# Attention stages of a two-block transformer: v as the stationary operand, and softmax division ahead of the transposes

## What is computed

```python
def mixer_a(q, k, v, qg, kg, rope):            # 8 heads, 2 kv heads, head width 64; mixer_b the same with window, bias, sink
    q = axial_rope(rmsnorm(q, qg), rope)
    k = axial_rope(rmsnorm(k, kg), rope)
        sc = jnp.einsum('bqkgd,bskd->bkgqs', qblk, k).astype(jnp.float32)
        p = jax.nn.softmax(sc, axis=-1).astype(v.dtype)
        return jnp.einsum('bkgqs,bskd->bqkgd', p, v)

def mixer_c(...):                              # 4 heads, two softmaxes each, v of width 128
    lam = (jnp.exp(jnp.sum(lq1 * lk1)) - jnp.exp(jnp.sum(lq2 * lk2)) + lambda_init)
        p = jax.nn.softmax(sc + bias[None, :, :, None], axis=-1)
        attn = p[:, :, :, 0] - lam * p[:, :, :, 1]
        return jnp.einsum('bkgqs,bskd->bqkgd', attn.astype(v.dtype), v)
    o = rmsnorm(o, subln_g) * (1.0 - lambda_init)
```

## Time and profile before

| | |
|---|---|
| three runs, median (lowest to highest) | 2922.46 us (2916.77 to 2925.27) |
| profiled execution, span | 2917.6 us |
| profiled execution, device time | not listed apart from its span |
| PE busy | 2663.8 us, 91% |
| DVE, ACT, POOL busy | 1366.9, 983.7, 189.3 us |
| a mixer, from half 3 to the next stage's transposed rows | 231.52 us, twice |

### The profile page before, as it was taken

How to read it: one execution, slowest core, us unless ns; L and a number is a source line. 1 busy time by engine, 2 the same in 40 slices (tenths; PEclk the granted TensorE clock), 3 DMA queues, 4 the chain that set the end, 5 groups by cost and what they waited for, 6 DMA issues and landing times.

```text
span 2917.6 us, 56415 instructions
## 1 busy us (share of the span) xinstructions
PE 2663.8 (91%) x24182; PEld 1779.7 (61%) x24182; DVE 1366.9 (47%) x1878; ACT 983.7 (34%) x1705; POOL 189.3 (6%) x195
## 2 busy tenths in 40 slices
PE   8999999999999999999999998899999989766666
PEld 6877877878878878875433333344778865332222
DVE  5776566877866567643100001423777773000001
ACT  4435655444446555531200100202555542000000
POOL 0102000000002000000000000002333310000000
PEclk9999999999999999999999999999999999987787
DMA  8764335776763347642899999822100017999997
GB/s 304 274 258 161 127 131 210 302 267 244 297 236 135 125 166 286 229 176 107 346 421 421 421 421 421 328 81 101 42 11 17 11 47 282 421 421 421 421 419 323
DMA packets 103997, 716.99 MB, mean 246 GB/s; under 512 B 11949, under 2 KB 14381, under 8 KB 19801
## 3 DMA queue, kind: packets, MB, share of 16 engines
q1 hardware_dynamic: 93016, 663.75, 57.8%
q10 hardware_dynamic: 10752, 49.81, 4.5%
HBM read 711.65 MB, written 1.86 MB: 245 GB/s over the span
## 4 chain that ended last, share of the span: by engine, by line
PE 61%; DMA 20%; DVE 10%; ACT 6%; issue 2%; SPq 0%; ACTq 0%; DVEq 0%
DMA weight_ring<-in_stream 20%; PE banks L2130 9%; PE banks L667 7%; PE banks L669 6%; PE banks L668 6%; PE banks L1960 3%; PE banks L2495 3%; PE banks L1103 3%; PE banks L1105 2%; PE banks L1104 2%; PE banks L2539 2%; ACT front L1371 2%; PE banks L1263 1%; PE banks L2935 1%; PE banks L2021 1%
## 5 line engine op out<-in xcount | busy, mean ns | idle before, releaser
L2130 PE MATMUL banks<-weight_ring,scratch 128*32 128x256 f32 (+1 forms) x4256 | 560.3, 507 | 148.6 <-DMA weight_ring<-in_stream 147.0
L2130 PEld LDWEIGHTS banks<-weight_ring,scratch 128*32 128x32 f32 (+1 forms) x4256 | 183.1, 129 | 505.9 <-DMA weight_ring<-in_stream 258.7
L664 DVE TENSOR_TENSOR split_high<-weight_ring,split_high 128x1024 fp32r<-128x1024 f32 x198 | 242.5, 1238 | 124.0 <-ACT split_high L659 121.8
L659 ACT CAST split_high<-weight_ring 128x1024 fp32r<-128x1024 f32 x198 | 206.8, 1052 | 272.8 <-PE banks L669 199.3
L2281 DVE TENSOR_TENSOR scratch<-scratch,banks 128x512 f32<-128x512 f32 (+1 forms) x32 | 17.8, 555 | 561.5 <-PE banks L2130 561.5
L1463 DVE TENSOR_TENSOR split_high<-weight_ring,split_high 128x1024 fp32r<-128x1024 f32 x128 | 160.2, 1262 | 160.9 <-ACT split_high L1356 160.8
L667 PE MATMUL banks<-split_high,features_low 128*128 128x512 f32 x480 | 189.9, 396 | 0.2 <-DVE resid L700 0.2
L669 PE MATMUL banks<-split_high,features_high 128*128 128x512 f32 x480 | 187.1, 390 | 0.0
L668 PE MATMUL banks<-split_high,features_high 128*128 128x512 f32 x480 | 186.8, 389 | 0.0
L1356 ACT CAST split_high<-weight_ring 128x1024 fp32r<-128x1024 f32 x128 | 133.0, 1049 | 150.1 <-PE banks L1105 144.2
L2190 ACT ACTIVATE scratch<-banks 128x512 f32<-128x512 f32 (+1 forms) x32 | 15.7, 491 | 477.7 <-PE banks L2130 477.7
(11 more groups left out here) (448 smaller groups left out, 4870.2 us busy)
## 6 DMA issues: line engine op xcount, KB each, us to landing
weight_ring<-in_stream SPq DMA_DIRECT2D x628, 1024.0 KB, 9.8
scratch<-in_kept ACTq DMA_DIRECT2D x24, 1024.0 KB, 7.6
scratch<-in_pair_rows ACTq DMA_DIRECT2D x8, 448.0 KB, 3.7
scratch<-in_kept ACTq DMA_DIRECT2D x6, 512.0 KB, 5.5
scratch<-in_lora ACTq DMA_DIRECT2D x2, 1536.0 KB, 9.3
front<-in_gain_rows ACTq DMA_DIRECT2D x5, 512.0 KB, 3.7
bias<-bias_rows SPq DMA_DIRECT2D x1, 2304.0 KB
scratch<-in_routing ACTq DMA_DIRECT2D x1, 1040.5 KB, 4.9
```

The lines of the kernel that those rows point to most:

```text
L659: act.copy(split[i % 4][0], source(i)).then_inc(*self.rounded.up())
L664: dve.tensor_tensor(lo, source(i), hi.bitcast(F32), ALU.subtract).then_inc(*self.rest.up())
L2130: last = pe.matmul(self.psum[q * M:(q + 1) * M, (GATE, UP, DOWN)[part], 0:W], left, w[j][:, q * W:(q + 1) * W], start=(k == 0), stop=(k == ...
```

## The change

On PE:
- `values` of A and B: v (128x64) is the loaded operand and the turned probabilities of four heads are streamed (512 columns): four products instead of 16. The two kv heads write to PSUM partitions 0 to 63 and 64 to 127 of bank 7. The result is already transposed, so the `turn_outs` of A and B fall away, and with them two entries of `starts` (35.5 and 49.5).
- `turn_probs` waits for `probs_normed` instead of `expd`; in C it has two groups instead of four, and `values` of C has 8 products instead of 16.

On DVE `norm_probs` is new and stands after `maxima`: in C it divides both softmaxes by their sums and combines them, in two groups; in A and B it only inverts the sums, in four groups. `outputs` of C is a plain copy; of A and B it makes the low part of the transposed outputs. On POOL sixteen groups of two `tensor_scalar` of 128x256 divide the probabilities of A and B in place. On ACT `high_outs` copies the high part after each phase of A and B, `high` and `low` of A and B fall away, the small exponentials stand ahead of the eight large ones, and C's are taken in the order 0, 4, 1, 5, 2, 6, 3, 7. `yT_hi` and `yT_lo` of A have room of their own. The host orders the rows of `w_branch` for A and B by pairs of heads.

```diff
             def turn_probs(ph):
                 fill(at_probs[ph])
-                for g in range(4):
-                    wait(pe, self.expd, 8 * ph + 2 * g + 2)
+                before = groups_before[ph]
+                for g in range(groups_of[branch_of[ph]]):
+                    wait(pe, self.probs_normed, before + g + 1)
                     if g >= 2:
-                        wait(pe, self.probs_saved, 4 * ph + g - 1)
+                        wait(pe, self.probs_saved, before + g - 1)
...
             def values(ph):
                 fill(at_values[ph])
...
+                if branch == "C":
+                    for i in range(4):
+                        if i % 2 == 0:
+                            wait(pe, self.probs_saved, before + i // 2 + 1)
+                        at = VC + P * (i // 2)
+                        for k in range(2):
+                            last = pe.matmul(self.psum[:, 7, i * P:(i + 1) * P], probsT[:, 2 * i + k, :], proj[:, k, at:at + P],
+                                             start=(k == 0), stop=(k == 1))
+                else:
+                    wait(pe, self.probs_saved, before + 4)
                     for k in range(2):
-                        last = pe.matmul(self.psum[:, bank, col:col + w], probsT[:, 2 * i + k, :], proj[:, k, at:at + w],
-                                         start=(k == 0), stop=(k == 1))
+                        for h in range(2):
+                            at = V0[branch] + HD * h
+                            last = pe.matmul(self.psum[HD * h:HD * h + HD, 7, :], proj[:, k, at:at + HD],
+                                             probsT[:, 8 * h + k:8 * h + 8:2, :], start=(k == 0), stop=(k == 1))
...
             turn_keys("B")
-            turn_outs("A")
...
             values(5)
-            turn_outs("B")
...
+            def high_outs(ph):
+                to(at_values[ph] + 3)
+                t = ph % 2
+                wait(act, self.attended, ph + 1)
+                act.copy(yT_hi[branch_of[ph]].rearrange("p (k c) -> p k c", k=4)[:, :, t * P:(t + 1) * P],
+                         self.psum[:, 7, :].rearrange("p (k c) -> p k c", k=4)).then_inc(*self.parts_high.up())
...
+            def norm_probs(ph):
+                branch, first = branch_of[ph], 8 * ph
+                if branch == "C":
...
+                    for g in range(2):
+                        wait(dve, self.expd, first + 4 * g + 4)
+                        mine, theirs = (slice(m + 2 * g, m + 2 * g + 2) for m in (0, 4))
+                        dve.reciprocal(rden[:, mine], den[:, mine]).then_inc(*ve.up())
+                        then(dve.reciprocal(rden[:, theirs], den[:, theirs]))
+                        then(dve.tensor_scalar(rden[:, theirs], rden[:, theirs], lam[:, 0:1], None, ALU.mult))
+                        for h in (2 * g, 2 * g + 1):
+                            ins = dve.tensor_scalar(probs[:, 4 + h, :], probs[:, 4 + h, :], rden[:, 4 + h:5 + h], None, ALU.mult)
...
+                        for h in (2 * g, 2 * g + 1):
+                            last = dve.scalar_tensor_tensor(out=probs[:, h, :], in0=probs[:, h, :], scalar=rden[:, h:h + 1],
+                                                            in1=probs[:, 4 + h, :], op0=ALU.mult, op1=ALU.add)
+                        last.then_inc(*self.probs_normed.up())
+                else:
...
+                    for g in range(4):
+                        mine = slice(2 * g, 2 * g + 2)
+                        wait(dve, self.expd, first + 2 * g + 2)
+                        if branch == "B":
+                            then(dve.tensor_tensor(den[:, mine], den[:, mine], snk[:, mine], ALU.add))
+                        then(dve.reciprocal(rden[:, mine], den[:, mine]))
+                        dens_inverted.append(ve.count)
...
             pool.tensor_tensor(v, v, bc(a_ri.rearrange("p (t h) -> p t h", t=TT), HD), ALU.mult).then_inc(*self.keys_normed.up())
+            for n in range(16):
+                pool.wait_ge(self.ve.sem, dens_inverted[n])
+                for i in (2 * (n % 4), 2 * (n % 4) + 1):
+                    last = pool.tensor_scalar(probs[:, i, :], probs[:, i, :], rden[:, i:i + 1], None, ALU.mult)
+                last.then_inc(*self.probs_normed.up())
```

154 lines of the change are left out of this document (76 added, 78 removed).

## The result

| | before | changed |
|---|---|---|
| device time, median (lowest to highest) | 2919.61 us (2915.50 to 2925.27), 4 runs | 2945.32 us (2941.81 to 2945.64), 4 runs |
| ratio, with its 95% interval | | 1.0086 (1.0068 to 1.0103) |
| profiled execution: span, device time | 2917.6 us, not listed | 2940.0 us, 2941.81 us |

The account below looks back on a forecast made before the run. PE, busy 91% of the span, was taken as the bound. Gains of 12.9 less losses of 5.2 and 0.2 us gave 7.5 per mixer, 15 in both: 2902.6 us span, plus 4.9 to the median, 2907.5 us; range 2898 to 2928.

Parts of the forecast that it names:

- p = 0.75 us: Assumed length of each POOL division in A and B, between 0.53 and 1.06 us; called the largest unknown.
- 32p - 18.8: Losses per mixer in us for other lengths p of POOL's operation; all gain gone at p = 0.99.
- I had this as a rival: POOL and DVE shut each other out: 3.6 us lost per mixer, 2914.5 us; chance 0.13.
- POOL is the new bound: In `turn_probs` of phases 2 to 5, POOL's operation takes 1.06 us: slower, 2927 us; chance 0.12.
- its dearer case: POOL's operation at 1.2 us with DVE in its way: 13 us more, 2936 us.
- All three signs of being wrong: POOL's operations over 0.9 us, PE's waits over 10 us in a mixer, or the mixer stretch not shrunk.
- The pairs don't overlap: `values` of A and B costs 3.7 us instead of 1.87: 2921.5 us, no change; chance 0.05.
- C's division is dearer: A group of C's division on DVE takes 3.2 us, not 2.1: 4.4 us per mixer, 2916 us; chance 0.08.
- PE's gains: Work and waiting PE loses in `values`, `turn_outs` and before half 52: 12.9 us per mixer.
- C's 3.5: `values` of C goes from 32 to 16 records: 1.75 us, twice, 3.5 us gained per mixer.
- no gain in C's `turn_probs`: Phases 0 and 1: shorter transposes gain 0 us, as the split of the next half is late instead.
- no wait before half 52: PE's wait of 1.16 us there goes because banks are long empty: 1.1 us gained per mixer.

Follow-up runs that it names:

- PE kept busy: The changed kernel with six idle products on PE ahead of the waits of the last three groups in phases 2 to 5; 2930.38 us, ratio 1.0040.
- without the division: The changed kernel with the division of A and B left out, DVE's reciprocals alone releasing the transposes; 2904.12 us, ratio 0.9947.
- C alone: The kernel before with only branch C's part of the change, DVE dividing and combining, A and B untouched; 2918.98 us, ratio 0.9988.

## Why the prediction was wrong

**The failed step is the price of POOL's operation, p = 0.75 us.** It measured 1.084 on average. The prediction's own formula, 32p - 18.8, gives 15.9 us per mixer for that, and the kernel with PE kept busy shows 15.7. Phase by phase its working with the measured durations gives 4.8, 2.7, 3.9 and 4.6 us, and the four stretches show 4.7, 3.1, 3.7 and 4.2. So the path through `turn_probs` was right, and its largest term was mis-sized, in three parts:
- I took a value between two rows, "nearest to the row of the same width", and that row was a `tensor_tensor`. A `tensor_scalar` costs 2.5 ns per column on POOL, a broadcast `tensor_tensor` 1.7. The copy of 128x512 in 0.66 us made me think columns with one input cheap; for this operation they aren't. The estimate of 0.4 us and more that the prediction took from the Trainium skill's one-input figure was further off still.
- The 128x128 row had a constant, as line 3485 shows, and the change a scalar per partition: 0.075 us. Together these give 0.531 + 128 x 2.5 ns + 0.075 = 0.926 us, where 0.928 was measured: 5.7 us per mixer over p = 0.75.
- DVE shuts POOL out. I had this as a rival, but with the wrong victim: I priced DVE's small inversions held up by POOL, and these cost nothing. What costs is POOL held up by DVE's low parts and gating, 5.0 us in four operations per mixer (0.75 + 1.97 + 1.79 + 0.51 over 0.928).

**A term was missing: PE's clock.** Nothing in the working said what PE's waits do to PE itself. Behind them the granted clock is at 1.2 GHz for 24 us of the first mixer and 27 of the second, and behind POOL's divisions alone that costs 6.5 us per mixer. With PE kept busy the change is 0.4% slower instead of 0.86% (2930.38 us).

The sum per mixer: forecast -7.5; p undisturbed +5.7; DVE +5.0; clock +6.5; this is +9.7. The trace shows +9.5 in the first mixer and +11.3 in the second, where half 22 adds 1.6 at the lower clock: 20.8 us in both. The span of the profiled execution grew by 22.4 us: the scan is 6.5 us longer than in the profile of before, the other stretches outside the mixers 4.9 shorter. The medians differ by 25.7 us, 4.9 more than the mixers account for, and the profile, which is of the fastest of the four runs, doesn't say where these are.

**By the rivals:** "POOL is the new bound" is what happened, with p = 1.084 beyond its break-even of 0.99. But it gave 2927 us for 1.06, and would give 2928.5 for 1.084 (15.9 - 12.9 = 3.0 per mixer), because it too had no clock in it. Even its dearer case, 2936 us for 1.2 "with DVE in its way", lies below what was measured. The upper end of my range, 2928, stood for p = 1.06. All three signs of being wrong that I had named came: operations over 0.9 us, waits over 10 us in a mixer, and a stretch that did not shrink. "The pairs don't overlap" fell (1.87 us), and so did "C's division is dearer" (a group takes 1.97 us from its first reciprocal to the next group's, and phase 0 13.83 us against 13.87).

**What was right:** PE's gains, 12.9 us per mixer forecast, 12.4 and 10.6 measured without the division; C's 3.5 (3.6 and 2.0 alone), both less in the second mixer by the slow half 22; no gain in C's `turn_probs`, with the low part of half 16 the last to end (a wait of 0.47 us); no wait before half 52 (96 products in 22.14 us without a gap).

## What to carry to other kernels

Price an instruction by a row with the same operation and the same kind of scalar, not by one of the same size, and if the break-even lies inside the bounds, look which engine's large operations run beside it. A wait on PE can cost more than its length: ask what the granted clock does behind it, and read it in the stretches after the wait, where PE is busy and nonetheless slow. Before a step is placed later, list what waits for its banks next: the half chunk in between was hiding an emptying.

## What was unexpected of the hardware

- GpSimd multiplies 128x512 by broadcast reciprocals in 1.041 us with `tensor_tensor`, but 128x256 with `tensor_scalar` in 0.928.
- One GpSimd operation of 0.93 us took 2.90 us beside two VectorE operations with both inputs in SBUF, and beside one whose large input was in PSUM 0.93.
- Six idle products ahead of each of three waits in phases 2 to 5 made the kernel 15 us faster: the clock stayed at 2.4 GHz there.
- Waits of 1.31 and 0.48 us in phase 1 had the lower clock behind them in one mixer of C alone, and not in the other.
- A scan of 11464 PE records that no edit touched took between 401 and 413 us. It was 4 to 7 us longer than in the kernel before when 2.6 us of work were put in 900 us ahead of it, and within the kernel's own two lengths when 5.2 us were.
